# HGRN level operands made under the last projections, kept in DRAM and read back by passes of seven

## The reference

```
log_f = logaddexp(log(lb), log1p(-lb) + log_sigmoid(fl));  k = (1 - lb) * sigmoid(-fl)
b = cumsum(log_f)                       # within a chunk, per channel
scores[t,s] = sum_k q[t,k] * k[s,k] * exp(b[t,k] - b[s,k])      for s <= t, else 0
o[t] = sum_s scores[t,s] * v[s] + (q[t] * exp(b[t])) @ state
```

## Time and profile before

| | us |
|---|---|
| median of 3 runs (lowest, highest) | 1367.6 (1365.52, 1374.32) |
| the profiled execution's own time | 1369.72 |
| its span in the profile | 1367.9 |
| TensorE busy | 1195.5 (87%) |
| VectorE busy | 492.1 (36%) |
| ScalarE busy | 395.5 (29%) |
| GpSimd busy | 175.8 (13%) |
| mean granted TensorE clock, share of full | 0.944 |

### The profile page before, as it was taken

How to read it: one execution, slowest core, us unless ns; L and a number is a source line. 1 busy time by engine, 2 the same in 40 slices (tenths; PEclk the granted TensorE clock), 3 DMA queues, 4 the chain that set the end, 5 groups by cost and what they waited for, 6 DMA issues and landing times.

```text
span 1367.9 us, 17632 instructions
## 1 busy us (share of the span) xinstructions
PE 1195.5 (87%) x7200; PEld 667.2 (49%) x7200; DVE 492.1 (36%) x1168; ACT 395.5 (29%) x754; POOL 175.8 (13%) x182
## 2 busy tenths in 40 slices
PE   5799999999999998887889988777759999999940
PEld 4444744447446897774554434345533333333310
DVE  5322314112840367665422222146641222221218
ACT  3202731113751332216671000365210111111115
POOL 1000011110000023431000000111001111111114
PEclk9899999999999998798999999899859999999975
DMA  5311112221211130001231003401129999999536
GB/s 174 108 31 32 31 55 73 75 74 46 62 62 38 40 72 33 2 33 35 89 117 38 0 0 128 184 32 47 45 103 415 413 418 414 425 415 415 231 140 260
DMA packets 65723, 184.88 MB, mean 135 GB/s; under 512 B 25588, under 2 KB 42212, under 8 KB 55908
## 3 DMA queue, kind: packets, MB, share of 16 engines
q1 hardware_dynamic: 57600, 166.71, 32.0%
q0 software_dynamic: 7456, 16.92, 3.2%
q10 hardware_dynamic: 580, 0.05, 0.0%
HBM read 165.29 MB, written 27.80 MB: 141 GB/s over the span
## 4 chain that ended last, share of the span: by engine, by line
PE 77%; DVE 9%; issue 6%; ACT 3%; POOL 2%; DMA 2%; ACTq 0%; DVEq 0%; POOLq 0%
PE bank L2263 28%; PE bank L1408 12%; PE bank L1469 7%; PE bank L1434 6%; PE bank L1484 2%; PE bank L1524 2%; PE bank L1394 2%; PE bank L2371 2%; PE bank L797 1%; PE bank L2252 1%; POOL arena L855 1%; PE bank L827 1%; PE bank L769 1%; POOL arena L856 1%; DVE arena L1655 1%
## 5 line engine op out<-in xcount | busy, mean ns | idle before, releaser
L2263 PE MATMUL bank<-arena 128*128 128x512 f32 (+3 forms) x1088 | 380.9, 511 | 1.6 <-DVE arena L2075 1.6
L2263 PEld LDWEIGHTS bank<-arena 128*128 128x128 f32 x1088 | 207.7, 192 | 169.6 <-issue 154.2
L1408 PE MATMUL bank<-arena 128*32 128x512 f32 x1536 | 171.1, 597 | 2.0 <-DVE arena L1187 2.0
L1855 ACT ACTIVATE arena<-bank 128x512 f32<-128x512 f32 (+1 forms) x64 | 33.0, 516 | 262.1 <-PE bank L2263 261.8
L1408 PEld LDWEIGHTS bank<-arena 128*32 128x32 f32 x1536 | 50.7, 111 | 117.1 <-issue 117.1
L1469 PE MATMUL bank<-arena 128*128 128x512 f32 x220 | 95.6, 592 | 0.0
L1434 PE MATMUL bank<-arena 128*32 128x512 f32 x768 | 87.4, 595 | 0.7 <-ACT arena L1096 0.7
L1196 DVE TENSOR_TENSOR arena<-arena,bank 128x256 f32<-128x256 f32 x25 | 10.5, 421 | 169.0 <-ACT arena L1092 162.4
L1469 PEld LDWEIGHTS bank<-arena 128*128 128x128 f32 x220 | 41.3, 190 | 49.7 <-issue 49.7
L1843 ACT ACTIVATE arena<-arena 128x1024 f32<-128x1024 f32 x26 | 27.4, 1054 | 126.5 <-DVE arena L1256 106.2
L1256 DVE TENSOR_TENSOR arena<-arena,bank 128x512 f32<-128x512 f32 x32 | 22.0, 688 | 112.3 <-PE bank L1469 87.8
(11 more groups left out here) (372 smaller groups left out, 1643.7 us busy)
## 6 DMA issues: line engine op xcount, KB each, us to landing
arena<-in_w_e_gu SPq DMA_DIRECT2D x27, 2048.0 KB, 14.5
arena<-in_w_e_dn SPq DMA_DIRECT2D x33, 1024.0 KB, 14.1
arena<-in_w_in SPq DMA_DIRECT2D x11, 1024.0 KB, 5.3
arena<-y_d SPq DMA_DIRECT2D x8, 1024.0 KB, 5.6
arena<-in_w_e_gu SPq DMA_DIRECT2D x6, 1024.0 KB
arena<-in_w_e_gu SPq DMA_DIRECT2D x12, 512.0 KB
pk_d<-arena SPq DMA_DIRECT2D x8, 640.0 KB, 2.9
arena<-in_x SPq DMA_DIRECT2D x8, 512.0 KB, 3.5
```

The source lines that it names most:

```text
L1408: ins = mm(bank[part, :], hgT[:, k, part], w_gu(es[i] % NB, k), start=(k == 0), stop=(k == KT - 1))
L1855: ins = nc.scalar.activation(dst, psum[PROJ_BANKS[u % 3]][0:rows, cols], ACT.Copy, scale=QK_SCALE if CHUNKS[UNITS[u][0]][1] == col["bq"] a ...
L2263: ins = mm(psum[PROJ_BANKS[u % 3]][0:rows, 0:n], lhs(k), rhs(k), start=(k == 0), stop=(k == KT - 1))
```

## The change

- `hgrn_differences` and `hgrn_products` replace `hgrn_level` and GpSimd's loop. VectorE makes all 28 levels, differences of k and then products of k - 2, right behind the scans; the two gains (2191) move behind the scans. All three steps work in place in a stage of 14 buffers (`STAGE`), two passes of seven.
- ScalarE has the 28 exponentials ahead of its evacuations 10 to 15, 3 before `last(10)` and 5 more before each next one.
- `store_levels` on SP stores the seven operands of a pass to a new DRAM tensor `hz_d` in two DMAs (1280 and 512 KB, or 512 and 1280) and waits for them, four times. VectorE's first difference of pass 2 and of pass 3 waits for the store of pass 0 and 1; GpSimd's memsets ahead of GDN's block loads wait for the last store.
- `load_levels` reads a pass back in one DMA of 1792 KB: pass 0 over the weight buffers once all units are evacuated (SP, ahead of the block loads of GDN's step 2), pass 1 and 2 once GDN's last step is done, pass 3 once the scores of pass 1 are. `hgrn_scores` waits for them instead of `h_z`.
- The `dd_d` stores move ahead of the last weight chunk. The second broadcast of `x_cb` waits for `h_dve` 5 only. Some semaphores are merged to free three of them.

```
-        hE = [view(o_w + i * HALF, HALF) for i in range(2)]
-        Z_AT = ([o_w + T + i * HALF for i in range(NL - 1)] + [o_tmp + 6912],
-                [o_tmp + i * HALF for i in range(NL)], [o_tmp + (NL + i) * HALF for i in range(NL)],
-                [o_tmp + i * HALF for i in range(NL)])
+        STAGE = [[o_tmp + i * HALF for i in (0, 1, 2, 3, 4, 7, 8)], [o_tmp + i * HALF for i in (5, 6, 9, 10, 11, 12, 13)]]
+        STAGE_RUNS = [((0, 5, 0), (5, 7, 7)), ((0, 2, 5), (2, 7, 9))]
+        Z_AT = [o_w, o_tmp, o_tmp + NL * HALF, o_tmp]
+        hz_d = nc.dram_tensor("hz_d", (T // HALF * CT, P, NL * HALF), f32, kind="Internal").ap()
...
         def act_hgrn_E(act, k):
-            act.wait_ge(s["h_E"], k + 1)
-            nc.scalar.activation(hE[k % 2], hE[k % 2], ACT.Exp).then_inc(s["h_Ee"], 1)
+            z = view(STAGE[k // NL % 2][k % NL], HALF)
+            act.wait_ge(s["h_E"], 2 * (k + 1))
+            nc.scalar.activation(z, z, ACT.Exp).then_inc(s["h_Ee"], 1)
...
+        def hgrn_differences(dve, v, k):
+            it, lv = k // NL, k % NL
+            c, hf, h = it // NHALF, it % NHALF, LEVELS[lv]
+            if k == 0:
+                dve.wait_ge(s["g_st"], 16 * NT)
+                dve.wait_ge(s["g_sc"], NT)
+            elif k == NL:
+                dve.wait_ge(s["g_st"], 16 * (NT + 2))
+            elif lv == 0:
+                dve.wait_ge(s["h_st"], 32 * (it - 1))
...
+            v.tensor_tensor(z[:, :, 0], mid, b[:, :, 0], ALU.subtract).then_inc(s["h_E"], 1)
+            v.tensor_tensor(z[:, :, 1], b[:, :, 1], mid, ALU.subtract).then_inc(s["h_E"], 1)
+        def hgrn_products(dve, v, k):
...
+            dve.wait_ge(s["h_Ee"], k + 1)
+            v.tensor_tensor(z[:, :, 0], z[:, :, 0], kk[:, :, 0], ALU.mult).then_inc(s["h_z"], 1)
+            v.tensor_tensor(z[:, :, 1], z[:, :, 1], qq[:, :, 1], ALU.mult).then_inc(s["h_z"], 1)
+        def store_levels(sp, it):
+            sp.wait_ge(s["h_z"], 2 * NL * (it + 1))
+            for l0, l1, at_t in STAGE_RUNS[it % 2]:
+                sp.dma_start(hz_d[it][:, l0 * HALF:l1 * HALF],
+                             arena[:, o_tmp + at_t * HALF:o_tmp + (at_t + l1 - l0) * HALF]).then_inc(s["h_st"], 16)
+            sp.wait_ge(s["h_st"], 32 * (it + 1))
+        def load_levels(sp, it):
+            sp.dma_start(arena[:, Z_AT[it]:Z_AT[it] + NL * HALF], hz_d[it]).then_inc(
+                s["h_l0"] if it % 2 == 0 else s["h_l1"], 16)
...
-                    pe.wait_ge(s["h_z"], 2 * NL * (it + 1))
+                    pe.wait_ge(s["h_l0"] if it % 2 == 0 else s["h_l1"], 16 * (it // 2 + 1))
...
             sp.wait_ge(s["x_cb"], 16)
+            sp.wait_ge(s["g_o"], NT)
+            load_levels(sp, 1)
+            sp.wait_ge(s["h_l0"], 16)
+            load_levels(sp, 2)
             sp.wait_ge(s["h_scr"], 4 * 4)
             for c in range(CT):
                 if c == 1:
+                    sp.wait_ge(s["h_dve"], 5)
                     sp.wait_ge(s["x_cb"], 32)
-                    sp.wait_ge(s["h_E"], NIT * NL)
...
+            sp.wait_ge(s["h_scr"], 8 * 4)
+            load_levels(sp, 3)
...
+            chunks_freed([(u, KT - 1) for u in LAST if u < END_OF[11]])
             sp.wait_ge(s["g_D"], 1)
...
-            sp.wait_ge(s["g_st"], 16 * (NT + 2))
+            chunks_freed([(u, KT - 1) for u in LAST if u >= END_OF[11]])
+            for it in range(NIT):
+                store_levels(sp, it)
             sp.wait_ge(s["g_mo"], 4)
...
             for n in range(NT - 2):
+                if n == 0:
+                    sp.wait_ge(s["unit_e"], len(UNITS))
+                    load_levels(sp, 0)
...
-            pool.wait_ge(s["g_st"], 16 * (NT + 2))
+            pool.wait_ge(s["h_st"], 32 * NIT)
...
-            last(10)
-            last(11)
-            act.wait_ge(s["l_dve"], 3)
-            for i in range(12, 16):
+            k = 0
+            for i in range(10, 16):
+                if i == 12:
+                    act.wait_ge(s["l_dve"], 3)
+                while k < min(3 + 5 * (i - 10), NIT * NL):
+                    act_hgrn_E(act, k)
+                    k += 1
                 last(i)
...
+            dve.wait_ge(s["h_dve"], 2)
+            dve.wait_ge(s["h_act"], 3)
+            for k in range(NIT * NL + 2):
+                if k < NIT * NL:
+                    hgrn_differences(dve, v, k)
+                if k >= 2:
+                    hgrn_products(dve, v, k - 2)
```

More of the change, by code:

```diff
@@ new lines, in hgrn_differences @@
+            v.tensor_tensor(z[:, :, 1], b[:, :, 1], mid, ALU.subtract).then_inc(s["h_E"], 1)
+        def hgrn_products(dve, v, k):
+            it, lv = k // NL, k % NL
+            part = slice(it % NHALF * HALF, (it % NHALF + 1) * HALF)
+            z = block_halves(view(STAGE[it % 2][lv], HALF), LEVELS[lv])
+            kk = block_halves(a_f[:, it // NHALF, part], LEVELS[lv])
+            qq = block_halves(a_q[:, it // NHALF, part], LEVELS[lv])
+            dve.wait_ge(s["h_Ee"], k + 1)
+            v.tensor_tensor(z[:, :, 0], z[:, :, 0], kk[:, :, 0], ALU.mult).then_inc(s["h_z"], 1)
+            v.tensor_tensor(z[:, :, 1], z[:, :, 1], qq[:, :, 1], ALU.mult).then_inc(s["h_z"], 1)
@@ L526, in act_tail @@
             for u in range(NU):
-                for k in levels_beside(u):
-                    act_hgrn_E(act, k)
                 if u >= 1:
@@ L594, in act_tail @@
             act_tail2(act, link, stats)
-        def levels_beside(u):
-            it, j = u // 4, u % 4
-            return [(it + 1) * NL + lv for lv in (2 * j, 2 * j + 1) if it < NIT - 1 and lv < NL]
         def act_hgrn_o(act, u):
@@ L841, in pool_tail @@
         def pool_tail(pool):
-            pool.wait_ge(s["h_act"], 3)
-            for k in range(NIT * NL):
-                it, lv = k // NL, k % NL
-                c, hf = it // NHALF, it % NHALF
-                pool.wait_ge(s["h_Ee"], k + 1)
-                if it == 1:
-                    pool.wait_ge(s["g_o"], NT)
-                elif it >= 2:
-                    pool.wait_ge(s["h_scr"], 16 * (it - 1))
-                part = slice(hf * HALF, (hf + 1) * HALF)
-                e, z = block_halves(hE[k % 2], LEVELS[lv]), block_halves(hz(it, lv), LEVELS[lv])
-                kk, qq = block_halves(a_f[:, c, part], LEVELS[lv]), block_halves(a_q[:, c, part], LEVELS[lv])
-                nc.gpsimd.tensor_tensor(z[:, :, 0], e[:, :, 0], kk[:, :, 0], ALU.mult).then_inc(s["h_z"], 1)
-                nc.gpsimd.tensor_tensor(z[:, :, 1], e[:, :, 1], qq[:, :, 1], ALU.mult).then_inc(s["h_z"], 1)
             fox_pool(pool)
@@ L1734, in _ @@
                 chunks_freed(FILL[n])
-            chunks_freed([(u, KT - 1) for u in LAST])
-            assert nxt[0] == len(CHUNKS)
             def expand(n, k, to, sem):
@@ L2188, in _ @@
             v.scalar_tensor_tensor(h_b, a_f, 0.0, h_b, ALU.min, ALU.subtract).then_inc(s["h_dve"], 1)
-            for c in range(CT):
-                dve.wait_ge(s["n_rms"], c + 1)
-                v.scalar_tensor_tensor(l_h[:, c], l_h[:, c], pcol[:, PC["gain"] + 4 + c:PC["gain"] + 5 + c],
-                                       n_sq[0][:, c], ALU.mult, ALU.mult).then_inc(s["l_dve"], 1)
             dve.wait_ge(s["h_dve"], 1)
@@ L2198, in _ @@
                     ins.then_inc(s["h_dve"], 1) if c * NT + n == NU - 1 else link(ins)
+            for c in range(CT):
+                dve.wait_ge(s["n_rms"], c + 1)
+                v.scalar_tensor_tensor(l_h[:, c], l_h[:, c], pcol[:, PC["gain"] + 4 + c:PC["gain"] + 5 + c],
+                                       n_sq[0][:, c], ALU.mult, ALU.mult).then_inc(s["l_dve"], 1)
+            dve.wait_ge(s["h_dve"], 2)
[5 more added lines that the diff above has]
+                    hgrn_products(dve, v, k - 2)
             def inverse(n, i):
```

46 lines of the change are left out of this document (17 added, 29 removed).

## The result

| | before | after |
|---|---|---|
| median of 4 runs each (lowest, highest), us | 1368.34 (1365.52, 1374.32) | 1346.22 (1345.33, 1349.81) |
| ratio, 95% interval | | 0.9834 [0.9814, 0.9854] |
| profiled execution, span | 1369.72, 1367.9 | 1345.35, 1343.5 |
| TensorE, VectorE, GpSimd busy | 1195.5, 492.1, 175.8 | 1187.0, 505.0, 130.8 |

The change is faster by 22 us, 1.7% by the ratio. Some names have moved: in the kernel after, scores are lines 736 and 739, values 750 and 753, masks 657, differences 475 and 476, products 486 and 487, exponentials 335, stores 493, loads 499, projections 2285 with their evacuation 1866, the memsets 1824 to 1827. In the rows TensorE has two records for a product: the 14 score products of a unit are x28.

A forecast was written before the change was run, and what follows sets the result against it. TensorE bounds the kernel by its order of work, but late operands stop it in the HGRN scores. Gains of 21.1 and 0.9 us less 0.3 give -21.7 from 1369.7 (1348.0) or median 1367.6 (1345.9): forecast 1346.5, range 1342 to 1358.

The forecast's parts named there:

- Bound: HGRN scores: bound by the two-buffer chain of VectorE difference, ScalarE exponential and GpSimd products, not by TensorE; 13.9 us of waits.
- Part 1: HGRN scores without the chain: from unit 3's scores to the last values 57.6 us instead of 78.7, gain 21.1.
- The split of 14.0 and 7.1: HGRN scores: of the 21.1 us gain, 14.0 are TensorE's stops and 7.1 the slow-clock restart after each.
- Reads: Operands read back for the HGRN scores: 5.7 us per 1792 KB transfer, each with 10 us of room.
- Part 2: GDN steps 3 to 6: pass 0's levels leave; VectorE's difference slowed beside GpSimd's product in step 4; gain 0.9 us.
- Part 3: Levels and stores under the projections: 1.40 us per level, last product at 434.6, no cost to TensorE or GDN's start.
- The 0.95 us per instruction: VectorE's level instructions under the projections: slow bound, said to stand only beside GpSimd; 0.42 us expected with GpSimd idle.
- Part 4: Small things: ScalarE's table load at Fox, second broadcast, earlier diagonal stores; cost 0, at most 1.3 us.
- A: Projections: slower pace or stores hold TensorE at unit 18; 6.2 us lost (1352.7) or 3.2 lost (1349.7); chance 0.2.
- B: Serial stores delay GDN's start: gain cancelled at 14.7 us per store, 1389 at 20, 1425 at 29; chance 0.05.
- C: HGRN scores: clock stays slow or a read causes a new stop; gain at most 14 us, 1354 to 1360; chance 0.1.
- Total: Whole kernel: -21.1 - 0.9 + 0.3 = -21.7 us, giving 1348.0 from the profiled execution, 1345.9 from the median; forecast 1346.5.

The follow-up runs named there:

- experiment 2: Kernel before, with the 56 products moved from GpSimd to VectorE directly behind the same group's differences, at the old places: 1404.37 us, ratio 1.0259.
- experiment 3: Kernel before, with products on VectorE at the old places, in place, each group's products one GDN step or unit later: 1378.66 us, ratio 1.0047.
- experiment 1: Kernel before, with TensorE multiplying constants during its three stops ahead of the scores of pass 1, 2 and 3: 1366.17 us, ratio 0.9975.
- experiment 6: Changed kernel, with the reads of pass 1 and 2 held back until pass 0's scores are done: 1357.04 us, ratio 0.9894 to the kernel before.
- experiment 7: Changed kernel, with eight unused GpSimd products of constants beside GDN's steps 3 and 4: 1348.57 us (1 run).
- experiment 4: Changed kernel, with the 56 products back on GpSimd and VectorE making the differences only: 1361.72 us, ratio 0.9948 to the kernel before.
- experiment 5: Changed kernel, with each pass stored a second time to DRAM and all waits for both copies: 1355.27 us, ratio 0.9903 to the kernel before.

## Why the prediction was right

Forecast 1346.5, measured 1346.2; by the step:

- *Bound*: right. Experiments 2 and 3 fed the stage later still and it took longer, experiment 1 separated stop and clock.
- *Part 1, 21.1 us from unit 3 to the end*: measured 78.7 - 57.3 = 21.4. The pitch is (585.18 - 534.46) / 12 = 4.23 where 4.25 stood. The split of 14.0 and 7.1 holds as a sum (the three units behind the stops are 7.2 us too long); taken alone the clock is worth 5.1 (experiment 1). Another 0.77 us was not forecast: what stands ahead of unit 3 is shorter too, 3.05 for 3.36 in the very first scores among it.
- *Reads*: the term was too small. 1792 KB take 8.1 us (median of 4), 42% more than the 5.7 of the rate fit, and 11.8 the one that was issued right behind another. The 6.2 us estimated from the fit in the Trainium skill, DMA: Bandwidth & Descriptors, on the anatomy of one DMA, is nearer and still short; the page gives that fit for DMAs that GpSimd issues, and these are SP's. The size costs nothing, since the room was over 10 us; experiment 6 shows what it costs without.
- *Part 2, 0.9 us*: measured 1.85 up to the first scores, of which step 4 is 1.06 (8.96 to 7.90 us), the last A U products 0.55 (1.65 to 1.10, at a higher clock), steps 2 and 6 0.1 each. The cause given, contention, holds with the addition of experiments 3 and 7: it costs TensorE time only together with the queued differences.
- *Part 3*: start of the levels 392.3 (393.4 forecast), pace 1.34 us per level (1.40), one gap of 1.52 (2), last product 431.5 (434.6), evacuation of unit 15 at 430.7 (433.8), store 3 in 6.4 us (5.7) and landed at 438.0 (440.3). The 0.95 us per instruction of the earlier trace rows never appears on VectorE when GpSimd is idle; experiment 4 brings it back at once.
- *Part 4*: ScalarE's table load comes at 594.1 and is hidden, as said. The diagonal stores take 3.1 us and not 8.3 once they are ahead of the weight load, so most of the 8.3 came from the load ahead of them; the prediction's sentence that it is the kind of delay of which the page warns is not borne out.
- *Rivals*: A did not happen (no wait near 436; experiments 5 and 4 make it happen, with 3.4 and 7.6 us of wait), B did not (all stores land within 8.2 us, 14.7 would have been needed), C did not (clock 1.00 from 531 to 592), though its price is now measured.
- *Total*: the spans differ by 24.4 where 21.7 stood, since GDN and the first units gave 1.7 us more and the projections 1.0 by scatter; the medians differ by 22.1. That the forecast came within 0.3 us is luck: from the span its own sum gives 1348.0, from the median 1345.9, and 1346.5 was chosen between them, while single runs of the changed kernel lie between 1345.3 and 1349.8.

## What to carry to other kernels

Work that makes the bounding engine stop belongs in an earlier stage where its engine is idle, even if that takes a round trip through DRAM: 7 MB out and back cost nothing here, because each transfer had more room than it took, and that room is what to check. Price a stop of TensorE at its length plus the slow work behind it (1.5 to 3.0 us here, but nothing behind the 2.93 us of experiment 5), but do not count on the second part alone, since an engine that restarts faster may only meet the next late operand. Moving the two-input products from GpSimd to VectorE paid here only together with a place in which VectorE had nothing else to do; leaving the products on GpSimd beside VectorE's differences made both slow.

## What the hardware did that I had not expected

- One GpSimd product of 0.72 us took 8.62 while VectorE ran differences back to back, and one VectorE difference of 0.42 took 4.51 while GpSimd ran products (experiment 4). Spans on GpSimd are rough, but both end within 0.7 us of the place where the other engine pauses.
- Reads of 1792 KB from DRAM took 8.1 us, stores of the same bytes 6.4 with an empty queue.
- With unchanged work, the stretch of cross-attention takes between 159.8 and 165.3 us and the granted clock differs with it (0.89 and 0.86 in the two windows above). That is more than the differences between several of these kernels, while the stretch from GDN's first state product to the last values repeats within 0.1 us.
